# A hybrid decoder trunk on one core: two of four xbc units of each SSD group as joined 512-column matmuls

## The reference, cut to what matters

```
z, xbc, dt = split(h @ w_in)
xbc = silu(causal_depthwise_conv(xbc, conv_kernel) + conv_bias)   # 4 taps
xs, bm, cm = split(xbc)
# per group: chunked scan, gives y
y = y * silu(z); y = rmsnorm per group; return y @ w_out
```

## Time and profile before

| | us |
|---|---|
| median of 3 runs | 1286.51 |
| lowest and highest | 1286.28, 1286.92 |
| the profiled execution | 1286.15 |
| its span on the core | 1284.3 |
| TensorE busy | 1273.5 (99%) |
| VectorE busy | 998.9 (78%) |
| ScalarE busy | 760.5 (59%) |
| GpSimd busy | 237.0 (18%) |

### The profile page before, as it was taken

The page is one execution under the profiler, slowest core; times in us unless marked ns, Lnnn a source line. Parts: engine busy times, 40 slices in busy tenths (PEclk is TensorE's granted clock), DMA queues, the critical chain, the costliest instruction groups (busy, mean ns, idle before and its releaser), DMA issues.

```text
span 1284.3 us, 23538 instructions
## 1 busy us (share of the span) xinstructions
PE 1273.5 (99%) x8074; PEld 1154.2 (90%) x8074; DVE 998.9 (78%) x1554; ACT 760.5 (59%) x1374; POOL 237.0 (18%) x311
## 2 busy tenths in 40 slices
PE   9999999999999999999999999999999999999997
PEld 8888888899999888888888888999999989888887
DVE  6888778897668888668888678998977767888754
ACT  6655554555556656545556447878865656565642
POOL 2433110122002111111111112024421201111111
PEclk9999999999999999999999999999999999999999
DMA  8556645655445556645556647644445544555660
GB/s 282 185 184 211 204 160 173 196 186 177 151 132 191 185 194 207 206 162 171 188 185 224 197 151 263 222 153 132 132 140 195 187 157 140 181 183 192 225 199 37
DMA packets 62806, 232.52 MB, mean 181 GB/s; under 512 B 6992, under 2 KB 7568, under 8 KB 62608
## 3 DMA queue, kind: packets, MB, share of 16 engines
q1 hardware_dynamic: 62080, 230.73, 54.8%
q10 hardware_dynamic: 656, 0.86, 0.2%
HBM read 230.49 MB, written 1.08 MB: 180 GB/s over the span
## 4 chain that ended last, share of the span: by engine, by line
PE 96%; DVE 2%; ACT 1%; issue 0%; DMA 0%; POOL 0%; ACTq 0%; DVEq 0%
PE bank L1419 94%; DVE w_lo L822 1%; DMA raw<-w_gu 0%; PE bank L1767 0%; PE bank L1579 0%; PE bank L1739 0%; DVE t L822 0%; ACT w_hi L400 0%; PE bank L1519 0%; DVE root_n L825 0%; DVE root_n L822 0%; PE bank L1794 0%; DVE rms_n L825 0%; DVE acc L822 0%; ACT gate L453 0%
## 5 line engine op out<-in xcount | busy, mean ns | idle before, releaser
L822 DVE TENSOR_TENSOR w_lo<-raw,w_hi 128x1024 fp32r<-128x1024 f32 (+2 forms) x403 | 524.0, 1303 | 42.7 <-ACT w_hi L400 41.4
L400 ACT ACTIVATE w_hi<-raw 128x1024 fp32r<-128x1024 f32 (+2 forms) x403 | 441.8, 1098 | 35.8 <-PE bank L1419 27.8
L1419 PE MATMUL bank<-h,w_hi 128*128 128x512 f32 (+1 forms) x1808 | 447.1, 385 | 0.5 <-DVE w_lo L822 0.3
L1419 PE MATMUL bank<-a,w_hi 128*128 128x256 f32 (+1 forms) x1878 | 386.7, 324 | 0.3 <-DVE w_lo L822 0.2
L1419 PEld LDWEIGHTS bank<-h,w_hi 128*128 128x128 f32 x1808 | 321.3, 189 | 54.5 <-DVE h L825 0.8
L1419 PEld LDWEIGHTS bank<-a,w_hi 128*128 128x128 f32 x1878 | 310.8, 190 | 24.8 <-issue 0.5
L1419 PE MATMUL bank<-a,w_lo 128*128 128x256 f32 x1280 | 260.6, 283 | 0.0
L1419 PEld LDWEIGHTS bank<-h,w_lo 128*128 128x128 f32 x1736 | 242.1, 190 | 16.7
L1419 PE MATMUL bank<-h,w_lo 128*128 128x256 f32 x1736 | 254.7, 282 | 0.0
L400 ACT ACTIVATE corr<-bank 128x256 f32<-128x256 f32 x239 | 91.1, 382 | 267.2 <-PE bank L1419 267.2
L1419 PEld LDWEIGHTS bank<-a,w_lo 128*128 128x128 f32 x1280 | 204.5, 191 | 4.8
(11 more groups left out here) (193 smaller groups left out, 1063.6 us busy)
## 6 DMA issues: line engine op xcount, KB each, us to landing
raw<-w_gu SPq DMA_DIRECT2D x174, 512.0 KB, 4.2
raw<-w_down SPq DMA_DIRECT2D x64, 704.0 KB, 4.2
raw<-w_xbc SPq DMA_DIRECT2D x32, 512.0 KB, 4.1
raw<-w_conv_in SPq DMA_DIRECT2D x24, 512.0 KB, 3.8
raw<-w_q SPq DMA_DIRECT2D x16, 512.0 KB, 4.4
raw<-w_k SPq DMA_DIRECT2D x16, 512.0 KB, 3.5
raw<-w_v SPq DMA_DIRECT2D x16, 512.0 KB, 3.5
raw<-w_o SPq DMA_DIRECT2D x16, 512.0 KB, 3.8
```

The source lines that it names most:

```text
L400: return nc.scalar.activation(out, in_, ACT.Copy, scale=scale)
L822: return nc.vector.tensor_tensor(out, a, b, op)
L1419: return nc.tensor.matmul(out, lhs, rhs, start=start, stop=stop, skip_group_check=check)
```

## The change

The first and the last unit of each group (q = 0 and q = 3, that is B and the second x) go from `unit` to `pair_unit`. The sum of the halves is made by VectorE in place: it reads the first half of the bank and `corr` and writes the first half of the bank, then signals xbc_sum. ScalarE's acc of those units waits for xbc_sum instead of unit_done, and the silu of the unit before moves ahead of acc. On VectorE the add stands before the split of the step at q = 0 and before the conv at q = 3.

```diff
+        XBC_JOINED = (0, 3)
+        def xbc_index(t):
+            return 2 * (t // 4) + XBC_JOINED.index(t % 4)
...
+            if name == "xbc":
+                pair_first["xbc"] = pair_count
+                pair_count += 2 * GROUPS
...
                     if G < GROUPS:
-                        act.wait_ge(unit_done, nx + t + 1)
-                        at_least(act, xbc_ready, t - 1)
+                        if q in XBC_JOINED:
+                            corr_copy(q, xbc_index(t), nx + t)
+                            if t:
+                                silu_xbc(*divmod(t - 1, 4))
+                            act.wait_ge(xbc_sum, xbc_index(t) + 1)
+                        else:
+                            act.wait_ge(unit_done, nx + t + 1)
+                            at_least(act, xbc_ready, t - 1)
                         nc.scalar.activation(acc[t % 2][:, :], bank[q][:, 0:SEQ], ACT.Identity, bias=col(C_SSDB, t),
                                              scale=col(C_SSDK, 4 * t + 3)).then_inc(conv_begun, 1)
-                    if 0 < t <= 4 * GROUPS:
+                    if 0 < t <= 4 * GROUPS and (q not in XBC_JOINED or t == 4 * GROUPS):
                         silu_xbc(*divmod(t - 1, 4))
...
+                    if G < GROUPS and q in XBC_JOINED:
+                        dve.wait_ge(corr_ready, pair_first["xbc"] + xbc_index(t) + 1)
+                        tt(bank[q][:, 0:SEQ], bank[q][:, 0:SEQ], corr[xbc_index(t) % 2][:, :], ALU.add).then_inc(xbc_sum, 1)
                     if t < SSD_UNITS and q != 3:
                         split(nx + t + AHEAD)
...
-                        unit(nx + t, free("xbc", t), KT, H_NORMED, a, True, True,
-                             ready=(nh_ready, -H_NORMED) if t == 0 else None)
+                        one_unit = pair_unit if q in XBC_JOINED else unit
+                        one_unit(nx + t, free("xbc", t), KT, H_NORMED, a, True, True,
+                                 ready=(nh_ready, -H_NORMED) if t == 0 else None)
```

More of the change, by code:

```diff
@@ L223, in trunk @@
         conv_begun, xbc_ready, y_added = (sem(n) for n in ("conv_begun", "xbc_ready", "y_added"))
+        xbc_sum = sem("xbc_sum")
         cb_done, cb_ready, bn_ready, m_ready = sem("cb_done"), sem("cb_ready"), sem("bn_ready"), sem("m_ready")
```

## The result

The changed kernel takes 1301.38 us (median of 4 runs, 1300.09 to 1302.72), the kernel before 1286.51: 14.9 us slower, a ratio of 1.0114 with a 95% interval of 1.0102 to 1.0127. The forecast was 1296.8 us, with a range of 1290 to 1300. The profiled execution took 1302.72 us, at the upper end of the four.

The account below looks back on a forecast made before the run. It took a closed VectorE-ScalarE ring of 15.71 us a group, not TensorE, as the bound: 4.29 us early plus 6.10 us in the ring, 10.39, less 0.08 slack, 10.3 later, so 1296.8 us; range 1290 to 1300.

Parts of the forecast that it names:

- What bounds the stage: xbc units: VectorE and ScalarE form a closed ring of 15.71 us a group; TensorE is held some 0.16 us.
- Rival (b): Not slower: TensorE is the bound, VectorE's 1.15 us idle a group swallows the adds; 1285.2 us; chance 0.09 with Rival (d).
- The saving on TensorE: Joined matmul form in 16 units: 0.08 us less a unit, 1.3 us in all, left out of the sum.
- Rival (d): The joined form brings TensorE nothing here; changes only Rival (b), to 1286.5 us; chance 0.09 together with it.
- The price of the add in the bank: VectorE's add writing PSUM: taken as 425 ns like the SBUF write, between 410 and 680 ns.
- Rival (c): The add in the bank is slow, 0.68 us: 4.2 us more, 1301.0 us; chance 0.05.
- The detour at q = 3: Steady groups: corr copy, add and two hand-overs lengthen the path by 0.88 us a group.
- Rival (a): ScalarE's detour hides, only VectorE's busy time counts: 5.4 us, 1291.9 us; chance 0.12, shared with absorbed early loss.
- The early groups: From t = 0 to group 2's q = 3 conv, where VectorE never stops: 4.29 us.
- The ring: VectorE-ScalarE round trip, G = 3 to 7: grows 1.22 us a group, 6.10 us; chance of the whole forecast 0.74.
- So only the 0.34 us counts: Steady q = 0: corr copy and acc are covered, so the joined unit costs only the add's 0.34 us on VectorE.
- TensorE's own saving turns into waiting: TensorE's 1.3 us saving becomes idle time and appears in none of the forecast figures.

Follow-up runs that it names:

- e2: Kernel before, 16 units joined on TensorE only, no corr copy or add, second halves of the sums left out: 1286.88 us, ratio 1.0002.
- e1: Changed kernel with units kept in the 24-matmul form; corr copies (scale 0.0) and adds stay: 1301.1 us, ratio 1.0107.
- e9: Kernel before with ScalarE's four xd copies moved from q = 2 to q = 3, behind acc and silu: 1285.05 us, ratio 0.9987.
- e12: As e11, but units of groups 0 to 2 stay in the 24-matmul form, 10 units joined: 1284.36 us, ratio 0.9982 to the kernel before.
- e4: Changed kernel with only the q = 3 units joined: 1294.12 us, against 1286.65 before.
- e13: Changed kernel, q = 0 add ahead of yoff, unit 13 multiplied twice, 8 y matmuls of groups 2 to 6 issued twice: 1297.35 us.
- e6: Changed kernel with VectorE's add moved from behind the yoff block to ahead of it: 1298.91 us.
- e5: Changed kernel with unit 13 multiplied twice and the 16 y matmuls of groups 2 to 6 issued twice: 1299.28 us, ratio 1.0097.
- e7: Changed kernel with ScalarE's q = 3 corr copy ahead of its split and the silu behind acc: 1296.44 us.
- e11: e9 with 16 units joined, q = 3 corr copy ahead of split, adds ahead of yoff (q = 0) and y scalings (q = 3): 1288.12 us.

## Why the prediction was right and where it failed

- **What bounds the stage**: right. TensorE, busy 99% by the page, was not the bound of this stage. e2 (cheaper TensorE, no gain), e1 (dearer ring, full loss) and e9 (ring opened, gain without any cheaper work) show it from three sides. Rival (b), that the kernel gets no slower, falls with the result, and e2 shows that TensorE's saving would not have arrived either.
- **The saving on TensorE**, 0.08 us a unit: right, and without effect in the change. Where TensorE is the bound it arrives: 15.52 against 15.37 us a group with two joined units (e9, e12). Rival (d) falls.
- **The price of the add in the bank**: 0.42 us taken, 0.428 measured. Rival (c) falls; that its 1301.0 us lies nearest to the result of all numbers of the prediction is chance.
- **The detour at q = 3**, 0.88 us: right (16.60 us groups in e4, the two gaps). Rival (a), that it hides, falls.
- **The early groups**, 4.29 us: right within 0.1 (4.20).
- **The ring**, 6.10 us: right (6.09 in e13).
- **"So only the 0.34 us counts" at q = 0**: wrong. That step looked at VectorE's queue and ScalarE's, not at GpSimd's, although yoff releases GpSimd's sum and the add now stands between yoff and the split. 0.43 us in four groups, about 1.9 us in the median. I had even used the row with a split of 1.67 us and allowed for a split or two falling otherwise, as a random disturbance; it was a matter of who starts first.
- **"TensorE's own saving turns into waiting"** and "nothing is given back": wrong in their price. The step took a wait of TensorE as costing its own length. In my own forecast TensorE was to be idle 1.5 us a group; I did not ask what it would do to its clock. The sum had no term for it; it was some 1.6 (e6 to e13) to 2.1 us (e5) in the median, 3.9 in the profiled execution. The range, drawn up to 1300 for a slow add, held neither of the two.

What stays open: why the clock fell after some waits and not after others. In the changed kernel it fell after waits of 2.72, 1.70 and 1.46 us and not after two of 1.44. The other traces show that the length of the wait does not decide it. In e1 a wait of 1.65 us in group 5 was followed by no lower clock and one of 1.64 us in group 6 was:

```profile
892.87:910.22 17.35, 15.71 (x132) 15.49 (x130) 15.43 (x29) 13.30 (x36) 6.88 (x16) 1.00 0.39 122
910.22:928.67 18.45, 16.81 (x129) 16.59 (x127) 15.52 (x28) 13.26 (x36) 6.88 (x16) 0.91 0.34 115
```

In e4 a wait of 1.89 us in group 3 was followed by none (granted 1.00), and of three waits of 1.21 to 1.22 us in e7 the last alone was (0.90 in group 7). So what the clock costs in one execution seems to be partly chance. Nothing was run that varies the wait alone.

## What to carry to other kernels

An engine that is busy 99% of the time may still be led by others: compare a stretch of its work where nothing waits with the same stretch in the steady state, and follow a gap on the second engine to what released it before calling it slack. When an instruction is put into a list, look at what the instruction ahead of it releases on every engine, since the new one gives those a head start. And a transfer of a sum from one engine to the next and back is worth its place: the same 16 copies and 16 adds cost 14.9 us over the kernel before in one order, and in another (e11, which also has the four xd copies one unit later) 1.7 us over the kernel before and 3.1 us over e9, the kernel with those four copies moved alone.

## What the runs showed of the hardware that I had not expected

- VectorE's fp32 add with both its input and its output in one PSUM bank takes as long (428 ns for 256 columns) as with the output in SBUF (425).
- When VectorE's 1024-column subtraction and GpSimd's 256-column sum overlap, the later one is held: 1.64 and 0.73 us with GpSimd first, 1.22 and 1.64 us with VectorE first.
- In the changed kernel TensorE's granted clock went from 2.4 to 1.2 GHz at once or within about 1.3 us after waits of 1.46 to 2.72 us and stayed there for some 3 us (7 in group 3), and more matmuls in the waits made the kernel faster (e5). Waits as long, up to 1.89 us (e4), were followed by no lower clock in other groups and kernels.
